# Recurrent mixer: output and low-rank products over the whole array, output norm over rows of tokens

## The chip, the cores and the metric

The kernel runs on one core of one Trainium2 chip. The metric is device time in microseconds. The kernel before took 5264.46 us, the median of three runs (5259.58 to 5285.39). The chip is driven by five engines that each work through their own queue in order and meet at semaphores: TensorE (PE, with its weight loads as PEld), VectorE (DVE), ScalarE (ACT), GpSimd (POOL) and SyncE (SP), which issues DMAs.

## The reference, cut to what matters

The program is a first block of hybrid layers and a second block with a differential attention, a recurrent mixer and a routed feed-forward part. The change touches the recurrent mixer alone: a scan over 256 context and 512 image tokens in two directions, 16 heads of 64, then a norm of each head's output.

```python
def rwkv_prepare(z, shift_w, w0, w_up, a0, a_up, k_k, k_a):
    ...
    r, k, v, wd, ad, gd = jnp.split(z, RW_SPLIT_IDX, axis=-1)
    w_log = -jax.nn.softplus(-(w0[...] + jnp.einsum('btr,drc->dbtc', jnp.tanh(wd), w_up))) - 0.5
    a = jax.nn.sigmoid(a0[...] + jnp.einsum('btr,drc->dbtc', ad, a_up))
    ...

def wkv_scan(s0, scan_in):
    def step(s, inp):
        w, kk, a, k, v, r = inp
        sa = jnp.einsum('dbhij,dbhj->dbhi', s, kk)
        s = s * w[..., None, :] - sa[..., :, None] * (kk * a)[..., None, :] + v[..., :, None] * k[..., None, :]
        return s, jnp.einsum('dbhij,dbhj->dbhi', s, r)
    return lax.scan(step, s0, scan_in)

def rwkv_post(y, r, k, v, gd, g_up, r_k, ln_g, ln_b):
    mu = jnp.mean(y, axis=-1, keepdims=True)
    var = jnp.mean(jnp.square(y - mu), axis=-1, keepdims=True)
    yn = ((y - mu) * lax.rsqrt(var + RW_LN_EPS)).reshape(B, T, C) * ln_g + ln_b
    bonus = jnp.sum(hs(r) * hs(k) * r_k, axis=-1, keepdims=True) * hs(v)
    return (yn.astype(r.dtype) + bonus.reshape(B, T, C)) * (jax.nn.sigmoid(gd) @ g_up)
```

`wd` and `ad` have 64 channels each, so the two low-rank products contract over 64. The mean and the variance are over the 64 channels of a head, for each token.

## The kernel before, in words

The function `rwkv_phase` is a stage of its own between two barriers. It works on units: 8 channel tiles `g` (128 channels, two heads) times 2 directions `d`, so 16 units `u = 2 g + d`. The 768 tokens are cut into 12 chunks of 64, of which the last 8 are image tokens with outputs. Inside a chunk the recurrence is solved with triangular products (`solve`, with X, Y, U and the matrix wAT), and from chunk to chunk a state wS is carried (`scan`).

The order is written out by hand. An outer loop runs iterations -2 to 17, an inner one 36 slots `k`, and every engine walks the same two loops and issues what its functions say for a slot. In iteration `i` unit `i` is built (`solve`, `fill`), unit `i-1` is scanned, unit `i+1` is prepared (low-rank products, exponentials), and in odd iterations from 3 on the tile `g = (i-3)/2` is finished (`final_product`, `final_steps`, `finals`). In even iterations the bonus, v and the key norm of a tile are computed. Nothing but this order and the semaphores decides when an instruction starts; an instruction that waits holds back all that stands behind it on its engine.

What a slot holds on TensorE: four products of `solve` (L1891 for U, L1902 for Z, or L1874 for the gram matrices in slots 0 to 2), then in slots 3 to 11 four of `fill` (L1917, L1922, L1927), then a piece of the scan. The scan takes three slots a chunk: slot 0 of the three gives W (L1942, and L1945 from wS), slot 1 gives N (L1949), slot 2 the new state (L1964, L1967) and, for the 8 image chunks, the output: L1958 from qr, L1959 from C (a part of the tile `gate_rows` in the profile) and L1970 from D. These three have 64 columns of weights, one for each token of the chunk, and write partitions 0 to 63 of bank 6. ACT copies W and N out (L2088, L2091) and U (L2072), DVE makes wS from the bank and the decayed wP (L2203, the first of a unit L2206) and does masked copies and transposes (L2215 to L2255). In slots 24 and 35 DVE takes four chunks of outputs over to `rows` (in the profile `y_rows`, 64 partitions x 1024: token in the chunk x chunk and channel), a copy for direction 0 (L2266), an addition for direction 1 (L2269).

The low-rank products (L1988) stand in slots 0, 2, 4 and 6. The weights of w lie in partitions 0 to 63 of `up` and those of a in 64 to 127, so each product contracts over 64 rows; ACT opens them with a sigmoid (L2121), and DVE sums the logs with a scan (L2278) in slot 3.

The output norm works on channels in partitions. In slot 9 eight transposes turn `rows` to 128 channels x 512 tokens (L2032), DVE copies it (L2354), a product with a block matrix of ones gives each head's sum in all its channels (L2037, slot 12), DVE subtracts (L2358) and squares (L2362), a second such product gives the variance (L2042, slot 16), ACT takes the root (L2167, slot 17), DVE two reciprocals (L2367, slots 18 and 20) and the product (L2370), then the scale and shift (L2373), the bonus (L2377) and the gate (L2383).

In the profile, tiles that lie in reused memory bear that memory's name: `x` stands for yb, sq, rk and ob, `arena` for the constants, up, wb, wk, wq and wV.

Of the kernel before, what the change touches and what calls it, by code (L numbers as in the profile page):

```python
# [11 lines left out]
ALU = mybir.AluOpType  # L12
# [3 lines left out]
P = 128  # L16
D = 1024
# [1717 lines left out]
def rwkv_phase(nc, T, R, lora, gd, ob_d):  # L1735
# [16 lines left out]
    bonus, rk, rows, yb, sq, ob = R["bonus"], R["rk"], R["rows"], R["yb"], R["sq"], R["ob"]  # L1752
# [26 lines left out]
    def r_slot(u):  # L1779
        return 1 + u % 3  # L1780

# [22 lines left out]
    def solve_step(k):  # L1804
# [6 lines left out]
             "s_ready", "y_ready", "norm_sums", "bonus_sums", "v_turned", "rows_turned", "mean_ready", "var_ready",  # L1811
             "gate_ready",
             "opened", "exps_ready", "q_widened", "y_preset", "u_copied", "bt_copied", "kt_copied", "w_copied",
             "n_copied", "s_copied", "s_decayed", "squared", "norm_roots", "v_copied", "ln_root",
             "sums_ready", "less_ready", "b_ready", "a_ready", "k_ready", "q_ready", "r_ready", "wb_ready", "wk_ready",
             "pl_ready", "y_opened", "at_ready", "d_ready", "x_opened", "x_done", "y_back", "y_final", "gram_k_read",
             "y_taken", "kr_ready", "kk_ready", "rk_ready", "bonus_ready", "yb_ready", "centred", "sq_ready",
             "normed", "inverse_ready", "ln_inverse", "scaled", "added", "ob_ready"]
    with Phase(nc, names) as (
            block, rk_loaded, v_loaded, up_loaded, ob_stored0, ob_stored1,  # L1820
            lora_up, gram_b, gram_k, b_turned, k_turned, u_ready, z_ready, w_ready, n_ready,
            s_ready, y_ready, norm_sums, bonus_sums, v_turned, rows_turned, mean_ready, var_ready,
            gate_ready,
            opened, exps_ready, q_widened, y_preset, u_copied, bt_copied, kt_copied, w_copied,
            n_copied, s_copied, s_decayed, squared, norm_roots, v_copied, ln_root,
            sums_ready, less_ready, b_ready, a_ready, k_ready, q_ready, r_ready, wb_ready, wk_ready,
            pl_ready, y_opened, at_ready, d_ready, x_opened, x_done, y_back, y_final, gram_k_read,
            y_taken, kr_ready, kk_ready, rk_ready, bonus_ready, yb_ready, centred, sq_ready,
            normed, inverse_ready, ln_inverse, scaled, added, ob_ready):
        ob_stored = (ob_stored0, ob_stored1)  # L1830

# [26 lines left out]
        def _(pe):  # L1858
# [71 lines left out]
            def scan(k, u):  # L1930
# [91 lines left out]
            def final_product(k, g, u):  # L2022
                if k == 9:
                    pe.wait_ge(y_taken, 4 * (g + 1))
# [10 lines left out]
                elif k == 12:  # L2035
                    pe.wait_ge(yb_ready, g + 1)
# [1141 lines left out]
```

## Time and profile before

| | |
|---|---|
| median of three runs | 5264.46 us |
| the profiled execution | 5262.22 us, span 5260.4 us |
| TensorE busy | 4544.4 us, 86% |
| DVE busy | 3151.8 us, 60% |
| ACT busy | 1603.0 us, 30% |
| POOL busy | 753.5 us, 14% |
| the mixer's stage | about 2408 to 3561 us of the span |
| granted clock, mean | 0.934 |

The page counts an engine busy only in its own instructions. A matmul in four-byte numbers is two passes, each with its weight load, so a group "x8" in the timeline is four products. Passes overlap at their ends, so a step is read from one start to the next and not from the durations. Slot 0 of the odd iteration read below starts at 2761.56 us, that of the next at 2830.88 and of the one after at 2899.09. The rows of idle time in brackets say what released the engine.

### The profile page before, as it was taken

To read this page: it belongs to the slowest core of one execution; us is meant where nothing else is said; L and a number is where in the kernel's file an instruction comes from. 1 tells how busy PE (TensorE), PEld (TensorE's weight loads), DVE (VectorE), ACT (ScalarE), POOL (GpSimd) and SP (SyncE) were. 2 spreads that over 40 slices of the span, in tenths; PEclk is the share of its full clock that TensorE was granted. 3 is DMA by queue.
4 is the path that set the end of the run, shared out by engine and by line. 5 is a ranking of instruction groups with operands and counts; after the bars stand their busy time and mean duration, and the time that the engine had idled before them with its cause. 6 is when DMAs were issued, how large, how long until landed. Compare 5 with 4: busy or idle time off the path is not lost. (4 is left out here: it accounts for less than half of the span.)

```text
span 5260.4 us, 56898 instructions
## 1 busy us (share of the span) xinstructions
PE 4544.4 (86%) x20568; PEld 3189.7 (61%) x20568; DVE 3151.8 (60%) x6333; ACT 1603.0 (30%) x3153; POOL 753.5 (14%) x671
## 2 busy tenths in 40 slices
PE   7978998978998997697999999998977777887787
PEld 5636886744885575486888888876763333333333
DVE  5563223564222557656677777743548888888886
ACT  3233342333432224213445444533211111111111
POOL 0000010000110000100000000001004445444443
PEclk9978999978999899898999999998989899989889
DMA  3102332201334410230000000005229999999998
GB/s 117 35 0 80 96 96 71 64 0 46 100 97 181 178 34 1 86 112 30 10 12 12 12 12 12 3 3 168 87 78 422 417 411 414 415 404 417 410 411 356
DMA packets 141383, 777.70 MB, mean 148 GB/s; under 512 B 18692, under 2 KB 23188, under 8 KB 73000
## 3 DMA queue, kind: packets, MB, share of 16 engines
q0 software_dynamic: 80224, 565.16, 26.3%
q1 hardware_dynamic: 60872, 208.82, 12.1%
q8 instruction: 168, 2.75, 0.2%
q14 instruction: 119, 0.97, 0.1%
HBM read 753.99 MB, written 19.92 MB: 147 GB/s over the span
## 5 line engine op out<-in xcount | busy, mean ns | idle before, releaser
L2809 PE MATMUL psum<-rows,diag 128*128 128x512 f32 x2048 | 1019.7, 656 | 296.5 <-ACT diag L2788 295.1
L2809 PEld LDWEIGHTS psum<-rows,diag 128*128 128x128 f32 x2048 | 420.2, 211 | 877.7 <-issue 877.4
L419 DVE TENSOR_TENSOR w_split_lo<-w_raw,w_split_hi 128x1024 fp32r<-128x1024 f32 (+1 forms) x316 | 379.4, 1209 | 648.5 <-ACT w_split_hi L406 644.1
L2699 POOL DMA_INDIRECT rows<-in_peer_uv,sel_idx x512 | 618.0, 1207 | 933.8 <-PE psum L2809 636.4
L2714 DVE SCALAR_TENSOR_TENSOR uh<-rows,h_rows 128x1024 f32<-128x1024 f32 x512 | 628.0, 1227 | 181.0 <-DMA rows<-in_peer_uv,sel_idx 152.0
L406 ACT CAST w_split_hi<-w_raw 128x1024 fp32r<-128x1024 f32 (+1 forms) x316 | 322.6, 1028 | 824.5 <-PE psum L357 457.7
L2781 ACT ACTIVATE g<-g 128x4 f32<-128x4 f32 x128 | 26.3, 205 | 1077.0 <-DVE g L2725 1077.0
L592 POOL TENSOR_TENSOR uT_lo<-normed_rows,uT_hi 128x512 fp32r<-128x512 f32 x64 | 82.9, 1295 | 1377.1 <-ACT uT_hi L568 1377.1
L1891 PE MATMUL psum<-X_wide,wAT_wide 128*128 128x128 f32 x1920 | 262.6, 280 | 1.9 <-DVE X_wide L2235 1.9
L1891 PEld LDWEIGHTS psum<-X_wide,wAT_wide 128*128 128x128 f32 x1920 | 235.1, 192 | 35.1 <-issue 30.9
L1902 PE MATMUL psum<-U_wide,Y_wide 128*128 128x128 f32 x1536 | 206.0, 277 | 0.0
L357 PE MATMUL psum<-hT_mlp_hi,w_split_hi 128*128 128x512 f32 x512 | 199.5, 390 | 2.2 <-DVE hT_mlp_lo L239 2.2
L1902 PEld LDWEIGHTS psum<-U_wide,Y_wide 128*128 128x128 f32 x1536 | 188.0, 192 | 19.0 <-issue 18.7
L357 PE MATMUL psum<-hT_mlp_lo,w_split_hi 128*128 128x512 f32 x512 | 199.2, 389 | 0.0
L357 PE MATMUL psum<-hT_mlp_hi,w_split_lo 128*128 128x512 f32 x512 | 199.2, 389 | 0.0
L357 PE MATMUL psum<-w_split_hi,uT_hi 128*128 128x512 f32 x512 | 199.2, 389 | 0.0
L357 PE MATMUL psum<-w_split_lo,uT_hi 128*128 128x512 f32 x512 | 199.2, 389 | 0.0
L357 PE MATMUL psum<-w_split_hi,uT_lo 128*128 128x512 f32 x512 | 199.2, 389 | 0.0
L2072 ACT COPY U_wide<-psum 128x512 f32<-128x512 f32 x240 | 140.6, 586 | 188.4 <-PE psum L1891 185.0
L2203 DVE SCALAR_TENSOR_TENSOR wS<-psum,pl,wP 128x128 f32<-128x128 f32 x160 | 54.9, 343 | 205.0 <-PE psum L1967 205.0
L2788 ACT ACTIVATE diag<-ident_sb,g 128x128 f32<-128x128 f32 x512 | 163.5, 390 | 36.7 <-DVE g L2730 36.7
L2432 POOL DMA_DIRECT2D merge_stage<-hT_spill x8 | 4.3, 539 | 1180.4 <-POOLq L168 1173.0
(492 smaller groups left out, 9291.2 us busy)
## 6 DMA issues: line engine op xcount, KB each, us to landing
w_raw<-in_w_in SPq DMA_DIRECT2D x120, 512.0 KB, 4.7
w_raw<-in_w_up SPq DMA_DIRECT2D x64, 512.0 KB, 4.5
w_raw<-in_w_down SPq DMA_DIRECT2D x64, 512.0 KB, 4.4
wbuf_mod<-in_w_mod SPq DMA_DIRECT2D x12, 2048.0 KB, 12.5
w_raw<-in_w_out SPq DMA_DIRECT2D x24, 512.0 KB, 5.0
w_raw<-in_peer_wq SPq DMA_DIRECT2D x16, 512.0 KB, 4.8
rows<-in_peer_uv,sel_idx POOLq DMA_INDIRECT x512, 13.0
w_raw<-in_w_branch_a SPq DMA_DIRECT2D x8, 512.0 KB, 4.6
```

The lines of the kernel that those rows point to most:

```text
L357: last = nc.tensor.matmul(psum[0:rows, bank, 0:cols], l_, r_, start=(start and c == 0 and j == 0), stop=(stop and c == len(pairs) - 1 and ...
L406: nc.scalar.copy(ring.hi[:, q % SPLIT_RING, :, 0:w], raw[:, q % raw_ring, :, 0:w]).then_inc(hi_ready, 1)
L419: nc.vector.tensor_tensor(ring.lo[:, q % SPLIT_RING, :, 0:w], raw[:, q % raw_ring, :, 0:w], ring.hi[:, q % SPLIT_RING, :, 0:w].bitcast(F32 ...
L592: return nc.gpsimd.tensor_tensor(uT.lo[:, k, :], squares[:, k % 2, :], uT.hi[:, k, :].bitcast(F32), ALU.subtract)
L1891: last = nc.tensor.matmul(psum[:, b, i * P:(i + 1) * P], flat(wAT[:, c]), flat(X[:, c]), start=True, stop=True)
L1902: last = nc.tensor.matmul(psum[:, b, i * P:(i + 1) * P], l_, r_, start=True, stop=True)
L2072: nc.scalar.copy(flat4(U[:, batch(b)]), psum[:, b, :]).then_inc(u_copied, 1)
L2203: nc.vector.scalar_tensor_tensor(wS[:], psum[:, 5, 0:P], scale, wP[:], ALU.mult, ALU.add).then_inc(s_copied, 1)
L2699: nc.gpsimd.indirect_dma_start(out=rows[:, n % RB, :], out_offset=None, in_=I["peer_uv"], in_offset=bass.IndirectOffsetOnAxis(ap=sel[:, t, ...
L2714: nc.vector.scalar_tensor_tensor(prod[:], rows[:, n % RB, 0:D], 1.0, h[:, t, :], ALU.mult, ALU.mult, accum_out=dots[:, (n // BATCH) % 2, s ...
L2788: nc.scalar.activation(diag[:, n % (2 * BATCH), :], ident[:], ACT.Copy, scale=g2[:, b % 2, i:i + 1]).then_inc(diag_ready, 1)
L2809: last = nc.tensor.matmul(psum[:, 2 * (t % 2) + half, :], diag[:, n % (2 * BATCH), :], rows[:, n % RB, D + half * NB:D + (half + 1) * NB], ...
```

## The change

Three things are done.

The three output products of a chunk get 128 columns of weights: those of the chunk and of the one behind it in memory (`two`). So qr, C and D get room for one chunk more, which POOL sets to zero at the stage's start; D moves to a tile of its own (`D_wide`). The products write all 128 partitions of bank 6, of which only the first 64 are read, as before.

The low-rank products contract over 128 rows: the weights of w are followed by 64 rows of zeros and those of a preceded by them, laid out so by the host, and `up` and its DMA have twice the size.

The output norm is taken on `rows`, with tokens in partitions, ahead of the transposes: sums of 64 columns by a DVE reduction (slot 1), times -1/64 (slot 2), added by a broadcast over rows (slot 3), squared on ACT (slot 4), reduced again (slot 6), root of the 64 x 16 statistics on ACT (slot 10), reciprocal (slot 11), product over rows (slot 14). The eight transposes then stand in slot 15, and the scale and shift reads their bank (slot 17). The two products with ones are gone. The gate product stays in slot 19.

```diff
+    def two(ap, u, c):
+        return ap[:, u % 2, c:c + 2].rearrange("p c t -> p (c t)")
...
+            nc.gpsimd.memset(qr[:, :, N_ALL:], 0.0).then_inc(pads_zero, 1)
...
-                        yy = psum[0:L_CH, 6, (x_ % 4) * P:(x_ % 4 + 1) * P]
-                        at = slice(c * L_CH, (c + 1) * L_CH)
+                        yy = psum[:, 6, (x_ % 4) * P:(x_ % 4 + 1) * P]
+                        at = slice(c * L_CH, (c + 2) * L_CH)
                         nc.tensor.matmul(yy, qr[:, r_slot(u), at], wS[:], start=True, stop=False)
-                        nc.tensor.matmul(yy, Cc[:, u % 2, x_], v, start=False, stop=False)
+                        nc.tensor.matmul(yy, two(Cc, u, x_), v, start=False, stop=False)
...
-                        last = nc.tensor.matmul(yy, Dd[:, u % 2, x_], wN[:], start=False, stop=True)
+                        last = nc.tensor.matmul(yy, two(Dd, u, x_), wN[:], start=False, stop=True)
...
-                nc.tensor.matmul(psum[:, 7, 0:hi - lo], up[64 * w:64 * w + 64, d, :], lora[64 * w:64 * w + 64, lo:hi],
-                                 start=True, stop=True).then_inc(lora_up, 1)
+                nc.tensor.matmul(psum[:, 7, 0:hi - lo], up[:, w, d, :], lora[:, lo:hi], start=True, stop=True
+                                 ).then_inc(lora_up, 1)
...
             def final_product(k, g, u):
-                if k == 9:
-                    pe.wait_ge(y_taken, 4 * (g + 1))
+                if k == 15:
+                    pe.wait_ge(rows_normed, g + 1)
...
-                elif k == 12:
-                    nc.tensor.matmul(psum[:, 7, :], cst["ones"][:], yb[:], start=True, stop=True
-                elif k == 16:
-                    nc.tensor.matmul(psum[:, 7, :], cst["ones"][:], sq[:], start=True, stop=True).then_inc(var_ready, 1)
                 elif k == 19:
-                    pe.wait_ge(ln_root, g + 1)
+                    pe.wait_ge(scaled, g + 1)
...
+                if k == 4:
+                    act.wait_ge(rows_centred, g + 1)
+                    nc.scalar.activation(rowsq, rows[:], ACT.Square).then_inc(rows_squared, 1)
+                elif k == 10:
+                    nc.scalar.activation(lnst[:, 3, :], lnst[:, 2, :], ACT.Sqrt, bias=cst["ln_eps"][0:L_CH],
...
+                if k == 1:
+                    nc.vector.reduce_sum(lnst[:, 0, :], grouped, AX.X).then_inc(row_sums, 1)
+                elif k == 3:
+                    nc.vector.tensor_tensor(grouped, grouped, each(lnst[:, 1, :]), ALU.add).then_inc(rows_centred, 1)
+                elif k == 6:
+                    nc.vector.reduce_sum(lnst[:, 2, :], rowsq.rearrange("p (g e) -> p g e", e=L_CH), AX.X
+                elif k == 14:
+                    nc.vector.tensor_tensor(grouped, grouped, each(lnst[:, 0, :]), ALU.mult).then_inc(rows_normed, 1)
+                elif k == 17:
                     dve.wait_ge(rows_turned, g + 1)
-                    nc.vector.tensor_copy(yb[:], psum[:, 7, :]).then_inc(yb_ready, 1)
...
-                    nc.vector.tensor_scalar(yb[:], yb[:], prm[:, g, 7:8], prm[:, g, 8:9], ALU.mult, ALU.add
+                    nc.vector.tensor_scalar(yb[:], psum[:, 7, :], prm[:, g, 7:8], prm[:, g, 8:9], ALU.mult, ALU.add
```

How the instructions move is seen in three places. The first is DVE's queue in slots 1 to 4 of an odd iteration, before the change (the run of masked copies and masks of the second and third block, then the first state wS, then the log sum of the next unit).

```order
L2223 STREAM_TRANSPOSE X_wide<-Y_wide 128x512
L2215 COPY_PREDICATED Y_wide<-arena,psum 128x512
L2217 TENSOR_TENSOR wAT_wide<-psum,arena 128x512
L2220 TENSOR_TENSOR gate_rows<-psum,arena 128x256
L2223 STREAM_TRANSPOSE X_wide<-Y_wide 128x512
L2206 TENSOR_SCALAR wS<-psum,pl 128x128
L2246 TENSOR_TENSOR wBT_wide<-psum,arena 128x512
L2278 SCALAR_TENSOR_TENSOR Lc_tile<-arena,dec_tile 128x768
L2282 TENSOR_TENSOR dec_tile<-Lc_tile,dec_tile 128x768
L2203 SCALAR_TENSOR_TENSOR wS<-psum,pl,wP 128x128
L2235 COPY_PREDICATED X_wide<-arena,psum 128x512
```

The same place after it; line numbers are those of the changed kernel, where L2223, L2225, L2231 and L2214 are the L2215, L2217, L2223 and L2206 of before.

```order
L2231 STREAM_TRANSPOSE X_wide<-Y_wide 128x512
L2366 TENSOR_REDUCE ln_stats<-y_rows 64x16
L2223 COPY_PREDICATED Y_wide<-arena,psum 128x512
L2225 TENSOR_TENSOR wAT_wide<-psum,arena 128x512
L2228 TENSOR_TENSOR D_wide<-psum,arena 128x256
L2231 STREAM_TRANSPOSE X_wide<-Y_wide 128x512
L2214 TENSOR_SCALAR wS<-psum,pl 128x128
L2369 TENSOR_SCALAR ln_stats<-ln_stats 64x16
L2254 TENSOR_TENSOR wBT_wide<-psum,arena 128x512
L2286 SCALAR_TENSOR_TENSOR Lc_tile<-arena,dec_tile 128x768
L2373 TENSOR_TENSOR y_rows<-y_rows,ln_stats 64x1024
L2290 TENSOR_TENSOR dec_tile<-Lc_tile,dec_tile 128x768
```

The reduction of `rows` now stands ahead of the third block's copy and of the first state, the small product with -1/64 behind the state, and the addition over `rows` between the log sum and the subtraction. The second place is TensorE's queue around the transposes of `rows`, before the change in slot 9.

```order
L1967 MATMUL psum<-wN,wbt_wide 128x128
L1891 MATMUL psum<-X_wide,wAT_wide 128x128 x4
L1917 MATMUL psum<-qr,arena 128x128 x4
L1942 MATMUL psum<-arena,wBT_wide 128x128
L1945 MATMUL psum<-wS,arena 128x128
L2032 MATMUL psum<-ident_sb,y_rows 128x64 x8
L1891 MATMUL psum<-X_wide,wAT_wide 128x128 x4
L1922 MATMUL psum<-ident_sb,arena 128x128 x4
L1949 MATMUL psum<-wW,Y_wide 128x128
L1891 MATMUL psum<-X_wide,wAT_wide 128x128 x4
```

After it, in slot 15 (L1902, L1956 and L1960 are the L1891, L1945 and L1949 of before, L1913 the L1902).

```order
L1980 MATMUL psum<-wN,wbt_wide 128x128
L1983 MATMUL psum<-wN,D_wide 128x128
L1902 MATMUL psum<-X_wide,wAT_wide 128x128 x4
L1953 MATMUL psum<-arena,wBT_wide 128x128
L1956 MATMUL psum<-wS,arena 128x128
L2045 MATMUL psum<-ident_sb,y_rows 128x64 x8
L1902 MATMUL psum<-X_wide,wAT_wide 128x128 x4
L1960 MATMUL psum<-wW,Y_wide 128x128
L1902 MATMUL psum<-X_wide,wAT_wide 128x128 x4
L1971 MATMUL psum<-wS,qr 128x128
```

The transposes have moved behind the last of the second level's Z products and an output product, to the third W product after; what stood between the two places is now ahead of them.

The third is ACT's queue in slots 4 to 6, before the change.

```order
L2078 COPY wbt_wide<-psum 128x512
L2091 COPY wN<-psum 128x128
L2095 ACTIVATE wP<-wS,pl 128x128
L2121 ACTIVATE aa_tile<-psum,arena 128x512
L2072 COPY U_wide<-psum 128x512
L2081 COPY wkt_wide<-psum 128x512
L2088 COPY wW<-psum 128x128
L2121 ACTIVATE aa_tile<-psum,arena 128x256
```

After it; L2100, L2126, L2077, L2086 and L2093 are the L2095, L2121, L2072, L2081 and L2088 of before.

```order
L2083 COPY wbt_wide<-psum 128x512
L2096 COPY wN<-psum 128x128
L2100 ACTIVATE wP<-wS,pl 128x128
L2126 ACTIVATE aa_tile<-psum,arena 128x512
L2172 ACTIVATE x<-y_rows 64x1024
L2077 COPY U_wide<-psum 128x512
L2086 COPY wkt_wide<-psum 128x512
L2093 COPY wW<-psum 128x128
L2126 ACTIVATE aa_tile<-psum,arena 128x256
```

The square of `rows` now stands ahead of the copies of U and of wkt in slot 5, without a table load before it.

## Rows read from the trace of the kernel before

**Rows 1.** Busy us in one stretch: PE, PEld, DVE, ACT, POOL; clock, DMA, GB/s.
```profile
2780.00:2850.00 70.00, 67.16 (x505) 57.68 (x504) 50.33 (x80) 33.24 (x74) 0.00 (x0) 1.00 0.01 5
```

**Rows 2.** TensorE's timeline, slots 19 to 22: start, us, engine, line, out<-in, shapes, count.
```profile
2803.11 1.02 PE L2045 MATMUL psum<-gd,arena 128*128 128x512 f32 x2
2803.97 1.05 PE L1902 MATMUL psum<-U_wide,Y_wide 128*128 128x128 f32 x8
2804.96 0.43 PE L1958 MATMUL psum<-wS,qr 128*64 128x128 f32 x2
2805.23 0.38 PE L1959 MATMUL psum<-arena,gate_rows 128*64 128x128 f32 x2
2805.54 0.49 PE L1964 MATMUL psum<-arena,wkt_wide 128*128 128x128 f32 x2
2805.86 0.39 PE L1967 MATMUL psum<-wN,wbt_wide 128*128 128x128 f32 x2
2806.18 0.43 PE L1970 MATMUL psum<-wN,gate_rows 128*64 128x128 f32 x2
2806.54 1.16 PE L1891 MATMUL psum<-X_wide,wAT_wide 128*128 128x128 f32 x8
2807.54 0.39 PE L1942 MATMUL psum<-arena,wBT_wide 128*128 128x128 f32 x2
...
2807.99 1.06 PE L1891 MATMUL psum<-X_wide,wAT_wide 128*128 128x128 f32 x8
2808.88 0.39 PE L1949 MATMUL psum<-wW,Y_wide 128*128 128x128 f32 x2
```

**Rows 3.** TensorE's timeline around one low-rank product.
```profile
2762.50 0.44 PE L1942 MATMUL psum<-arena,wBT_wide 128*128 128x128 f32 x2
2762.87 1.12 PE L1988 MATMUL psum<-lora,arena 64*128 64x512 f32 x2
2763.93 1.16 PE L1874 MATMUL psum<-qr,arena 128*128 128x128 f32 x8
```

**Rows 4.** Groups by line and shape: count, busy us, mean ns, idle before.
```profile
L1360 DVE TENSOR_REDUCE x<-head_squares 128x16 f32<-128x1024 f32 x10 | 12.1, 1211 | 0.0
...
L2367 DVE RECIPROCAL x<-x 128x256 f32<-128x256 f32 x16 | 27.4, 1720 | 3.0 <-ACT x L2167 3.0
...
L1336 ACT ACTIVATE head_squares<-arena 128x1024 f32<-128x1024 f32 x6 | 6.3, 1054 | 1.9 <-DVE arena L2864 1.9
...
L1964 PEld LDWEIGHTS psum<-arena,wkt_wide 128*128 128x128 f32 x352 | 52.7, 189 | 19.2 <-issue 19.2
...
L1958 PEld LDWEIGHTS psum<-wS,qr 128*64 128x64 f32 x256 | 24.5, 134 | 17.3 <-DVE y_rows L2266 2.6
```

**Rows 5.** TensorE's timeline, slot 3, the W product behind the first state.
```profile
2769.79 0.49 PE L1945 MATMUL psum<-wS,arena 128*128 128x128 f32 x2 [0.32 <-DVE wS L2206]
```

**Rows 6.** DVE's timeline, slots 12 to 14.
```profile
2789.78 0.73 DVE L2235 COPY_PREDICATED X_wide<-arena,psum 128x512 f32<-128x512 uint32 x1 [0.54 <-PE psum L1902]
...
2793.98 0.68 DVE L2358 SCALAR_TENSOR_TENSOR x<-psum,x 128x512 f32<-128x512 f32 x1
...
2795.19 0.33 DVE L2203 SCALAR_TENSOR_TENSOR wS<-psum,pl,wP 128x128 f32<-128x128 f32 x1
...
2796.07 0.65 DVE L2362 TENSOR_TENSOR x<-x 128x512 f32<-128x512 f32 x1
```

**Rows 7.** TensorE's timeline, slot 27 of an odd and slot 33 of an even iteration.
```profile
2819.46 0.49 PE L1945 MATMUL psum<-wS,arena 128*128 128x128 f32 x2 [0.97 <-DVE wS L2203]
...
2896.39 0.49 PE L1942 MATMUL psum<-arena,wBT_wide 128*128 128x128 f32 x2
2897.03 0.49 PE L1945 MATMUL psum<-wS,arena 128*128 128x128 f32 x2
```

**Rows 8.** The timeline of all engines at the mixer's end.
```profile
3547.24 0.70 PE L2032 MATMUL psum<-ident_sb,y_rows 64*128 64x64 f32 x8 [0.77 <-DVE y_rows L2269]
...
3559.82 0.69 DVE L2383 TENSOR_TENSOR x<-x,psum 128x512 f32<-128x512 f32 x1
```

More of the change, by code:

```diff
@@ L1751, in rwkv_phase @@
     wS, wP, wW, wN, pl = R["wS"], R["wP"], R["wW"], R["wN"], R["pl"]
-    bonus, rk, rows, yb, sq, ob = R["bonus"], R["rk"], R["rows"], R["yb"], R["sq"], R["ob"]
+    bonus, rk, rows, yb, ob = R["bonus"], R["rk"], R["rows"], R["yb"], R["ob"]
+    rowsq, lnst = R["rowsq"], R["lnst"]
     def cells(ap):
@@ L2102, in widen_q @@
                 at = slice(64 * half, 64 * half + 64)
-                nc.scalar.copy(wq[at, u % 2, :, half, :], cells(qr[at, 0, :])).then_inc(q_widened, 1)
+                nc.scalar.copy(wq[at, u % 2, :, half, :], cells(qr[at, 0, 0:N_ALL])).then_inc(q_widened, 1)
             def preset(j, u):
@@ L2164, in final_steps @@
             def final_steps(k, g):
-                if k == 17:
-                    act.wait_ge(var_ready, g + 1)
-                    nc.scalar.activation(sq[:], psum[:, 7, :], ACT.Sqrt, bias=cst["ln_eps"][:], scale=1.0 / 64
-                                         ).then_inc(ln_root, 1)
+                if k == 4:
+                    act.wait_ge(rows_centred, g + 1)
+                    nc.scalar.activation(rowsq, rows[:], ACT.Square).then_inc(rows_squared, 1)
+                elif k == 10:
+                    act.wait_ge(row_vars, g + 1)
+                    nc.scalar.activation(lnst[:, 3, :], lnst[:, 2, :], ACT.Sqrt, bias=cst["ln_eps"][0:L_CH],
+                                         scale=1.0 / 64).then_inc(row_roots, 1)
             for i in ITERATIONS:
@@ L2844, in second_block_program @@
     gd = sbt("gd", [P, S])
-    arena = sbt("arena", [P, 13400])
+    arena = sbt("arena", [P, 13656])
     with ExitStack() as stage:
@@ L2923, in second_block_program @@
         cst = {n: share.take(list(I["rwc_" + n].shape)[1:]) for n in T["rwc_names"]}
-        R = {"cst": cst, "prm": share.take([DC, 10]), "up": share.take([2, P]), "gup": share.take([DC, P]),
+        R = {"cst": cst, "prm": share.take([DC, 10]), "up": share.take([2, 2, P]), "gup": share.take([DC, P]),
              "zr_d": z_d["r"], "zk_d": z_d["k"], "zv_d": z_d["v"]}
@@ L2995, in second_block_program @@
         R["ob"] = room[:, 2 * S:4 * S].rearrange("p (i n) -> p i n", i=2)
-        R["rk"], R["yb"], R["sq"] = (room[:, i * S:(i + 1) * S] for i in (4, 5, 6))
+        R["rk"], R["yb"] = (room[:, i * S:(i + 1) * S] for i in (4, 5))
+        R["rowsq"] = room[0:L_CH, 6 * S:8 * S]
+        R["lnst"] = sb("ln_stats", [L_CH, 4, 2 * XCH])
         room2 = T["gate_rows"][:].rearrange("p t d -> p (t d)")
-        R["C"], R["D"] = (room2[:, i * 2 * S:(i + 1) * 2 * S].rearrange("p (i c t) -> p i c t", i=2, t=L_CH)
-                          for i in range(2))
+        R["C"] = room2[:, 0:2 * (XCH + 1) * L_CH].rearrange("p (i c t) -> p i c t", i=2, t=L_CH)
+        R["D"] = sb("D_wide", [P, 2, XCH + 1, L_CH])
         rwkv_phase(nc, T, R, lora, gd, obT_d)
@@ L3127, in lay_out @@
     W = A["w_in_2"]
+    none = np.zeros((64, 2, DC * P), W.dtype)
     order = np.concatenate([W[:, :, 0:6144], W[:, :, 6400:8448]], axis=2)
@@ L3143, in lay_out @@
                                A["rw_ln_b_2"][0]], 1).reshape(DC, P, 9)),
-        "rw_up": c(np.concatenate([A["rw_w_up_2"][0].transpose(1, 0, 2), A["rw_a_up_2"][0].transpose(1, 0, 2)], 0)
-                   .reshape(P, 2, DC, P).transpose(2, 0, 1, 3)),
+        "rw_up": c(np.stack([np.concatenate([A["rw_w_up_2"][0].transpose(1, 0, 2), none], 0),
+                             np.concatenate([none, A["rw_a_up_2"][0].transpose(1, 0, 2)], 0)], 1)
+                   .reshape(P, 2, 2, DC, P).transpose(3, 0, 1, 2, 4)),
         "rw_gup": c(A["rw_g_up_2"][0].reshape(P, DC, P).transpose(1, 0, 2)),
```

66 lines of the change are left out of this document (32 added, 34 removed).

## The prediction

> **What bounds it now.** I read the page's shares first, then the stretches, then the timeline of one iteration of the recurrent mixer. The program is one core and the mixer runs from 2408 to 3561 us of its span; nothing else runs beside it, so a microsecond taken from it is one off the end. In that stage the reader is to see TensorE busy 67.16 of 70.00 us with DVE at 50.33, ACT at 33.24 and a granted clock of 1.00 (the upper of its two levels, 2.4 GHz) [rows 1]. TensorE is the bound, by its own queue: an iteration of 36 slots takes about 68 to 69 us and has no long idle stretch. But a share is a mean: DVE has 72% over the stretch and runs without a pause in some slots, and there its order decides (below). The sum is made against the profiled execution: 5262.22 us, span 5260.4, 2.2 us below the median of 5264.46.
>
> **The pace of TensorE, full and cut.** Products over the whole array start 0.22 us apart (two in the 0.45 us from 2807.54 to 2807.99) and a group of four takes 0.89 (2807.99 to 2808.88) [rows 2]. Around a product with 64 columns of weights it is slower. The slot from 2803.97 goes 0.99 for the group of four, then 0.27, 0.31, 0.32, 0.32, 0.36 for the five products of the scan, and 1.00 for the next group: 3.57 us up to 2807.54, where seven steps at the full pace are 0.89 + 5 x 0.22 + 0.89 = 2.88 [rows 2]. Every step into, inside or out of the narrow shape costs 0.05 to 0.14, though the narrow product does less. Difference 0.69 us.
>
> **The change, part by part.**
>
> (a) Output products with 128 columns. Eight slots of each scan have the three products; seven look like rows 2, the last (slot 35, nothing behind it in the scan) I take at 0.25. 7 x 0.69 + 0.25 = 5.1 us an iteration, for the 15 iterations that also build: 76 us. The added columns go to rows of the bank that nobody reads, and the copy out of it is still of 64 rows, so DVE pays nothing. In the last scan (no build) TensorE waits for the copies of the state at each hop; I count nothing there (0 to 5).
>
> (b) Low-rank products with 128 rows. 2762.50 to 2762.87 is 0.37 for a product that has 0.22 at full pace, the 512-wide product takes 1.06 against 0.86 for the full one at 2803.11, and the group after it is slowed as in rows 2, by 0.10 [rows 2, 3]: 0.15 + 0.20 + 0.10 = 0.45 each. Four an iteration, 15 iterations (the narrower ones taken alike): 27 us. The weights' DMA doubles from 128 KB; it is asked for an iteration early, so 0.
>
> The Trainium skill speaks against this part: "TensorE: Matmul & The Clock Gate", section "Why this matters for your kernels", gives a single matmul with 32 rows the same time as one with 128 and puts the gain in running several at once. By it (a) and (b) would be near zero. The rows above differ from that here, since what they show is a cost of the neighbours too.
>
> (c) Two ones products leave, 0.86 each (2803.11 to 2803.97) [rows 2], in the seven iterations that hold a final and a build: 12 us.
>
> (d) DVE and ACT of the output norm. Off DVE go the copy (0.69), the subtraction, the square, two reciprocals of 1.72 [rows 4] and the product, 6.2 us. On come four passes over 64 x 1024: none is in the trace. Bounds: the reduction of 128 x 1024 to 16 at 1.21 above [rows 4], and the 64 x 512 cut of it, half, below; I take 1.2, since time follows the free size. With three small ones of 16 columns (an estimate of 0.5 together) it is 5.3 us. So DVE's load is as before; what matters is where they stand. The skill's "VectorE: DVE Perf Modes", "Rules for kernel authors", calls the reduce the slowest DVE operation and advises restructuring. The row has it at 1.21, the price of any pass of that size; by the page alone the same sum would carry a longer stop in slot 1.
>
> (e) The tail. From the transposes at 3547.24 to the end of DVE's last product (3559.82 + 0.69) [rows 8] it is 13.3 us of pure chain. After: reduce, small, add, square, reduce, root, reciprocal, product, transposes, scale, gate product (2.1 us at the idle clock), multiply: about 11.3. Gain 2.
>
> Gross: 76 + 27 + 12 + 2 = 117 us.
>
> **What is late next.** TensorE's queue gets faster, and in these places it then meets DVE or ACT:
>
> - Slot 3, every iteration. TensorE already waits 0.32 for DVE's first state [rows 5]; DVE's run up to it starts after the previous output and is not shortened. The two low-rank products ahead of it save 0.9 that is lost again: 15 x 0.9 = 13.5.
> - Slot 1, seven iterations: the reduce stands in that same run ahead of the state: 1.15 each, 8. Behind it on DVE are the third block's masks and the state, which the scan's W product waits for.
> - Slot 4: ACT's Square waits for the centred rows, and behind it are the copies of U and of wkt, which TensorE needs for the next gram product. The Square has 1.05 [rows 4]. Bounds 0 and 1.7; TensorE is itself 1.15 late by then, so I take 0.5: 3.5.
> - Slot 15, seven iterations. DVE's block from 2789.78 ends its state copy at 2795.52, 5.7 later; without the subtraction at 2793.98 it is 5.1 [rows 6]. TensorE at full pace is there after 0.44 + 1.11 + 1.99 + 1.11 = 4.65. Then the transposes wait for the last row product: 2796.07 less 0.6 plus 1.2 is 6.9 after the zero, against 4.8. Wait 2.1, with the state's 0.5 in it. 7 x 2.1 and 0.5 for the first: 15. With the old order the transposes stood in slot 9 and waited for nothing.
> - Slot 27: the wait of 0.97 [rows 7] is DVE's and grows by the 0.7 that the slot saves, 8 odd iterations: 5.5.
> - Slot 33 of the even ones, behind the reciprocals of the key norm: 0.64 where the pace is 0.22 [rows 7]; what the last two slots save is lost: 0.9 x 7 = 6.5.
>
> Sum given back 52. Net 117 - 52 = 65: **5262 - 65 = 5197 us**.
>
> **Rivals.**
> - The new waits hardly show: a late TensorE lets DVE and ACT catch up, so that only the waits that show now (20 us: slots 3 and 33) grow: 5262 - 117 + 20 = 5165. For it: DVE at 72%; against it: rows 5 and 6 are in-order queues.
> - The row statistics cost more than their places: all of the first reduce, add and second reduce (3.6), the Square (1.05) and the Sqrt's table load at slot 10 (1.3) reach TensorE, with the 2.1 of slot 15: 7 x 8 = 56, and 32 of the other waits: 117 - 88 = 29, 5233. For it: DVE has no pause in slots 0 to 4; against: TensorE's own lateness covers part of each.
> - Padding gives nothing (the rule above): the slow steps belong to the place, not to the shape. Then gross is 14, waits 8 + 3.5 + 7 x 1.4 = 21: 5270, no change.
> - Slower: the weight load shows. A load of 64 columns takes 0.13, one of 128 0.19 [rows 4]; if the steps of rows 2 are loads that nothing covers, each of the 768 passes of (a) costs 0.058 more: +44, with the 27 of new waits of the norm and less 14: 5262 + 57 = 5319. It decides from the point where a slot of (a) saves less than 0.1 us (the rest, 41 against 52, is then a loss). Against it: at the full pace 128-column weights come every 0.11 us a pass, faster than the narrow ones.
>
> **From cases to numbers.** Forecast 0.59 (its own range 5170 to 5225), hidden waits 0.15, dearer statistics 0.13, no gain 0.08, slower 0.05. The range of 8 in 10 is 5160 to 5240. What a measurement can tell from no change is about 0.5%, 26 us: faster than 5238 is the forecast, the hidden waits and three quarters of the third case, 0.84; the same 0.11; slower 0.05.
>
> **What would show it.** Right: the scan's products of a y slot 0.22 apart and 2.9 us for the stretch of rows 2; the low-rank product 0.86; new idle time of TensorE before the first W product (about 2 us), before the transposes of the normed rows (up to 2) and the release of both by DVE; iterations of about 63 us (even) and 66 (odd). Wrong: the narrow steps unchanged with 128 columns (no gain), a lower granted clock in the stage, TensorE's waits over 8 us in an odd iteration, or a later start of the low-rank products.

## The result, and the profile after

The changed kernel took 5216.59 us (median of four runs, 5212.29 to 5219.81) beside 5266.03 for the kernel before (now the median of four); the ratio is 0.990 with a 95% interval of 0.9872 to 0.9927, which is 38 to 67 us. The forecast was 5197 with a range of 5160 to 5240: the time lies inside it and the change is faster, by 49 us between the medians where 65 were forecast. The profiled execution took 5219.48 us, span 5217.7, 42.7 below the one of before.

The page of the changed kernel, span and the engines' busy time:

```profile
span 5217.7 us, 56829 instructions
...
PE 4469.1 (86%) x20536; PEld 3204.8 (61%) x20536; DVE 3144.6 (60%) x6333; ACT 1604.5 (31%) x3161; POOL 751.5 (14%) x674
```

The share of TensorE is still 86%. What changed is seen in the timeline. The stretch that answers to [rows 2], slots 19 to 21 of an odd iteration (columns as there):

```profile
2923.74 1.02 PE L2050 MATMUL psum<-gd,arena 128*128 128x512 f32 x2
2924.60 1.05 PE L1913 MATMUL psum<-U_wide,Y_wide 128*128 128x128 f32 x8
2925.49 0.39 PE L1971 MATMUL psum<-wS,qr 128*128 128x128 f32 x2
2925.71 0.39 PE L1972 MATMUL psum<-arena,gate_rows 128*128 128x128 f32 x2
2925.93 0.39 PE L1977 MATMUL psum<-arena,wkt_wide 128*128 128x128 f32 x2
2926.16 0.39 PE L1980 MATMUL psum<-wN,wbt_wide 128*128 128x128 f32 x2
2926.38 0.39 PE L1983 MATMUL psum<-wN,D_wide 128*128 128x128 f32 x2
2926.60 1.06 PE L1902 MATMUL psum<-X_wide,wAT_wide 128*128 128x128 f32 x8
2927.50 0.39 PE L1953 MATMUL psum<-arena,wBT_wide 128*128 128x128 f32 x2
```

The narrow steps are gone. From 2924.60 the group of four takes 0.89, each of the five products 0.22, the next group 0.90: 2.90 us where it was 3.57, and 2.88 was the forecast.

Single passes show what the narrow shape cost. In the trace of before a pass starts 0.11 us behind the one ahead of it in either shape. Only at the border is it more: the first narrow pass comes 0.09 later than that, the one behind it 0.05, the first wide pass again 0.09 and the one behind it 0.10. A visit to the narrow shape costs 0.34 us, and the slot of [rows 2] has two. The low-rank product, the answer to [rows 3]:

```profile
2748.75 0.44 PE L1953 MATMUL psum<-arena,wBT_wide 128*128 128x128 f32 x2
2749.03 1.02 PE L2001 MATMUL psum<-lora,arena 128*128 128x512 f32 x2
2749.89 1.05 PE L1885 MATMUL psum<-qr,arena 128*128 128x128 f32 x8
```

0.28 into it and 0.86 for it, where it was 0.37 and 1.06. Pass by pass it is the same picture: 0.09 to 0.10 more at each of four steps (into the first pass, to the second, to the group behind, and to that group's second pass), and the same for the products with 256 columns as for those with 512. The first state of a unit now holds TensorE for longer, the answer to [rows 5]:

```profile
2888.57 0.49 PE L1956 MATMUL psum<-wS,arena 128*128 128x128 f32 x2 [2.22 <-DVE wS L2214]
```

And this is the place in slot 15 where the transposes now stand:

```profile
2914.13 0.49 PE L1956 MATMUL psum<-wS,arena 128*128 128x128 f32 x2 [0.55 <-DVE wS L2211]
2915.84 0.81 PE L2045 MATMUL psum<-ident_sb,y_rows 64*128 64x64 f32 x8 [1.23 <-DVE y_rows L2383]
2916.58 2.07 PE L1902 MATMUL psum<-X_wide,wAT_wide 128*128 128x128 f32 x8
2918.45 0.63 PE L1960 MATMUL psum<-wW,Y_wide 128*128 128x128 f32 x2
2918.88 1.45 PE L1902 MATMUL psum<-X_wide,wAT_wide 128*128 128x128 f32 x8
2920.16 0.39 PE L1971 MATMUL psum<-wS,qr 128*128 128x128 f32 x2
```

TensorE waits 0.55 for the state and 1.23 for the last product over rows, 1.78 in all where 2.1 was forecast. But then the group of four takes 1.87 us (2916.58 to 2918.45) and the next 1.28, where 0.89 is the pace. The granted clock falls in just this stretch; each row is a stretch of 1 us with the busy time of PE, PEld, DVE, ACT and POOL, the granted clock, the DMA share and GB/s:

```profile
2914.00:2915.00 1.00, 0.49 (x2) 0.30 (x2) 1.00 (x3) 0.27 (x1) 0.00 (x0) 1.00 0.00 0
2915.00:2916.00 1.00, 0.16 (x2) 0.16 (x3) 0.78 (x1) 0.00 (x0) 0.00 (x0) 1.00 0.00 0
2916.00:2917.00 1.00, 1.00 (x10) 0.88 (x10) 0.00 (x0) 0.00 (x0) 0.00 (x0) 0.64 0.06 16
2917.00:2918.00 1.00, 1.00 (x6) 1.00 (x6) 0.00 (x0) 0.00 (x0) 0.00 (x0) 0.50 0.00 0
2918.00:2919.00 1.00, 1.00 (x7) 1.00 (x6) 0.00 (x0) 0.31 (x1) 0.00 (x0) 0.50 0.00 0
2919.00:2920.00 1.00, 1.00 (x8) 1.00 (x8) 0.00 (x0) 1.00 (x4) 0.00 (x0) 0.65 0.00 0
2920.00:2921.00 1.00, 1.00 (x11) 1.00 (x11) 0.00 (x0) 0.84 (x2) 0.00 (x0) 1.00 0.00 0
```

The granted clock is 1.00 through the two waits and falls to 0.50, the lower of the two levels (1.2 GHz), once TensorE is busy again; the time at the lower level in these rows adds up to 3.4 us. The wait of slot 3 was followed by such a fall in six odd iterations and in one not. Iteration 5, behind a wait of 2.21, and iteration 7, behind the 2.22 shown above:

```profile
2757.00:2761.00 4.00, 3.83 (x28) 3.36 (x29) 4.00 (x6) 3.23 (x8) 0.00 (x0) 1.00 0.01 2
...
2889.00:2892.00 3.00, 3.00 (x16) 3.00 (x15) 3.00 (x4) 2.06 (x4) 0.00 (x0) 0.50 0.00 0
```

DVE's side of the norm, minimum, median and maximum in ns for eight instructions each:

```profile
L2366 DVE TENSOR_REDUCE ln_stats<-y_rows x8: 1165/1169/1211, 2619.3 to 3504.5; 64x16 f32<-64x1024 f32 x8
...
L2373 DVE TENSOR_TENSOR y_rows<-y_rows,ln_stats x8: 1187/1194/1216, 2625.1 to 3505.9; 64x1024 f32<-64x1024 f32 x8
...
L2386 DVE TENSOR_SCALAR x<-psum,arena x8: 800/802/811, 2657.3 to 3512.5; 128x512 f32<-128x512 f32 x8
```

The reduction and the pass over rows were taken at 1.2 and are 1.17 and 1.19. The scale that now reads the bank takes 0.80. And the end of the stage:

```profile
3503.74 0.68 DVE L2277 TENSOR_TENSOR y_rows<-y_rows,psum 64x512 f32<-64x512 f32 x1 [2.27 <-PE psum L1983]
...
3511.38 1.11 PE L2045 MATMUL psum<-ident_sb,y_rows 64*128 64x64 f32 x8 [7.67 <-DVE y_rows L2383]
...
3515.56 0.69 DVE L2396 TENSOR_TENSOR x<-x,psum 128x512 f32<-128x512 f32 x1 [1.50 <-PE psum L2050]
```

From the end of the output's copy (3504.42) to the end of the last product (3516.25) it is 11.8 us; 11.3 was forecast, against 13.3 before.

The start of slot 0 in each iteration gives a ruler that the rest of the program does not disturb. In the table the even and the odd iteration are iterations 10 and 9, and the sum runs from slot 0 of iteration 0 to slot 0 of iteration 15, so that it holds six of the seven odd iterations with a build and a final. The time of a run is its median, and the ratio is to the kernel before on the same chip.

| kernel | time us | ratio (95%) | even | odd | sum of 15 |
|---|---|---|---|---|---|
| before | 5264 to 5268 | | 68.20 | 69.33 | 1014.0 |
| changed | 5216.6 | 0.990 (0.9872 to 0.9927) | 63.60 | 69.27 | 975.5 |
| low-rank alone | 5246.6 | 0.9961 (0.9947 to 0.9974) | 67.08 | 68.36 | 999.0 |
| output products alone | 5219.8 | 0.9915 (0.9901 to 0.9928) | 64.71 | 67.39 | 973.1 |
| both of these | 5205.9 | 0.9882 (0.9866 to 0.9897) | 63.58 | 66.61 | 960.0 |
| norm over rows alone | 5270.0 | 1.001 (0.9996 to 1.0023) | 68.21 | 69.85 | 1018.9 |
| changed, waits filled | 5203.7 | 0.9867 (0.9845 to 0.9888) | 63.59 | 66.29 | 959.0 |
| changed, norm late | 5181.0 | 0.9828 (0.981 to 0.9846) | 63.58 | 63.15 | 939.2 |
| norm late, wk late | 5168.1 | 0.9802 (0.9784 to 0.982) | 63.40 | 62.10 | 929.7 |
| before, narrow products together | 5250.1 | 0.9957 (0.9941 to 0.9974) | 66.61 | 68.71 | 996.6 |

The first rows say it at once: the even iterations got 4.6 us shorter, the odd ones, in which the norm stands, hardly at all (0.06). Not every odd iteration of the changed kernel is like the ninth: iterations 3 to 13 took 70.65, 67.81, 69.20, 69.27, 69.27 and 69.08 us.

### The profile page after: what moved, and what is told of

The parts are those of the page before. It is cut to its first block and busy times, and to the rows that moved or that the text cites. A ratio compares the mean times of both kernels' runs of the same rounds, so it can differ in the third digit from the quotient of the medians.

```text
span 5217.7 us, 56829 instructions
## 1 busy us (share of the span) xinstructions
PE 4469.1 (86%) x20536; PEld 3204.8 (61%) x20536; DVE 3144.6 (60%) x6333; ACT 1604.5 (31%) x3161; POOL 751.5 (14%) x674
## 5 line engine op out<-in xcount | busy, mean ns | idle before, releaser
L1902 PE MATMUL psum<-X_wide,wAT_wide 128*128 128x128 f32 x1920 | 266.6, 284 | 1.7 <-DVE X_wide L2243 1.4
L1902 PEld LDWEIGHTS psum<-X_wide,wAT_wide 128*128 128x128 f32 x1920 | 248.8, 200 | 17.5 <-issue 13.6
L1913 PE MATMUL psum<-U_wide,Y_wide 128*128 128x128 f32 x1536 | 202.2, 275 | 0.0
L1913 PEld LDWEIGHTS psum<-U_wide,Y_wide 128*128 128x128 f32 x1536 | 188.8, 192 | 7.5 <-issue 6.5
L2077 ACT COPY U_wide<-psum 128x512 f32<-128x512 f32 x240 | 140.1, 584 | 165.1 <-PE psum L1902 161.5
```

What stands on the lines that cost most here:

```text
L1902: last = nc.tensor.matmul(psum[:, b, i * P:(i + 1) * P], flat(wAT[:, c]), flat(X[:, c]), start=True, stop=True)
L1913: last = nc.tensor.matmul(psum[:, b, i * P:(i + 1) * P], l_, r_, start=True, stop=True)
L2077: nc.scalar.copy(flat4(U[:, batch(b)]), psum[:, b, :]).then_inc(u_copied, 1)
```

## The experiments

**The output products alone.** Of the diff only these lines, with the zeroed room behind qr, C and D that they need.

```diff
-                        yy = psum[0:L_CH, 6, (x_ % 4) * P:(x_ % 4 + 1) * P]
-                        at = slice(c * L_CH, (c + 1) * L_CH)
+                        yy = psum[:, 6, (x_ % 4) * P:(x_ % 4 + 1) * P]
+                        at = slice(c * L_CH, (c + 2) * L_CH)
...
-                        nc.tensor.matmul(yy, Cc[:, u % 2, x_], v, start=False, stop=False)
+                        nc.tensor.matmul(yy, two(Cc, u, x_), v, start=False, stop=False)
...
-                        last = nc.tensor.matmul(yy, Dd[:, u % 2, x_], wN[:], start=False, stop=True)
+                        last = nc.tensor.matmul(yy, two(Dd, u, x_), wN[:], start=False, stop=True)
```

> The kernel before with the output products at 128 columns of weights and nothing else. Theory A (the ledger: narrow products slow TensorE's queue by 0.69 us a slot, waits on DVE take some of it back, the full change lost its last 20 us to the norm and to falls of TensorE's clock after its waits): gross 76, given back about 16 in slots 15, 27 and 33, so 60 us faster than before, about 5204, faster than the whole change; no stretch at the lower clock in the odd iterations; even and odd iterations both near 64.5 us. Theory B (each part gives its share of the 46 measured, padding 40 of it): 40 faster, about 5225.

44 us faster, not 60. The steps of 0.22 are there and, in iterations 3 to 14, the full clock, and the whole change is not better than this part alone (5219.8 and 5216.6). The expected 64.5 came for the even iterations; the odd ones have 67.4. There TensorE meets DVE in slots in which the forecast had no wait. TensorE's waits in the second half of an odd iteration, slots 21, 26 and 27:

```profile
2931.15 0.49 PE L1955 MATMUL psum<-wS,arena 128*128 128x128 f32 x2 [0.43 <-DVE wS L2215]
...
2934.42 0.49 PE L1970 MATMUL psum<-wS,qr 128*128 128x128 f32 x2 [0.77 <-DVE y_rows L2278]
...
2938.35 0.49 PE L1955 MATMUL psum<-wS,arena 128*128 128x128 f32 x2 [1.43 <-DVE wS L2215]
```

The first (0.43) stands behind the reciprocals of the old norm, the second (0.77) waits for the copy that empties the output bank, the third (1.43) for the state. Together 2.6 us, where the forecast had one wait of 1.67 in slot 27. Set beside the trace of before product by product, an even iteration here gains 4.9 us in its eight output slots and gives 1.4 back to waits; the odd one gives back about 3.0 of the same gain. Theory B's number was nearer here, but its reasoning (parts that add up) does not fit the ruler: the three parts alone are 41, 15 and -5 us in the sum of 15 iterations, together 51, and the changed kernel has 38.5. In the times the two cannot be told apart (44, 17 and -6 make 55, within the interval of 38 to 67).

**The low-rank products alone.**

```diff
-                nc.tensor.matmul(psum[:, 7, 0:hi - lo], up[64 * w:64 * w + 64, d, :], lora[64 * w:64 * w + 64, lo:hi],
+                nc.tensor.matmul(psum[:, 7, 0:hi - lo], up[:, w, d, :], lora[:, lo:hi], start=True, stop=True
```

> The kernel before with the low-rank products over 128 rows and nothing else. Theory A: 27 us gross, the half that stands ahead of slot 3's W product is lost to the wait for DVE's first state, which grows from 0.32 to about 1.2 us: 12 to 14 faster, about 5252. Theory B (a product over 64 rows has the price of one over 128, and only the steps around it count): 4 to 6 faster, about 5260, with the 512-wide product itself still at 1.06 us.

15 us less in the sum of 15 iterations and a ratio of 0.9961, which is 20 us with an interval of 14 to 28 (the medians differ by 17). The profiled execution was the slowest of the five (5266.8), so only the mixer's stage is read from it. TensorE's wait for the first state in this kernel:

```profile
2900.69 0.49 PE L1945 MATMUL psum<-wS,arena 128*128 128x128 f32 x2 [0.89 <-DVE wS L2206]
```

0.89 where it was 0.32: 0.57 of what the two products ahead of it saved is lost in that wait, as (b) had it. Each iteration gains 1.0 to 1.1 us; 0.9 was the forecast. Theory B's numbers are out: the gain is three to four times as large, and the 512-wide product now has 0.86 by its starts. Its thought is not: the 0.20 that the product is shorter is 0.10 and 0.09 at the border of its two passes, the same for 512 and for 256 columns, so this too can be a price of changing shape rather than of a product over 64 rows. No run has such products one behind the other.

**The norm over rows alone.** The statistics on rows, the transposes in slot 15 and no ones products, as in the diff of the change; the paddings left out.

> The kernel before with the output norm over rows of tokens and nothing else. Theory A: 12 us of ones products and 2 of the tail go, the waits in slots 3 and 15 cost 8 + 3 + 8, and TensorE's clock falls to half after them in most of the seven odd iterations, 1.5 us each time: 5 to 25 us slower than before, 5270 to 5290. Theory B (the norm over rows is worth its two products, the whole change lost its time elsewhere): 5 to 12 faster, about 5256.

0.1% slower with an interval from no change to 0.2%: the lower end of theory A's time, and against theory B's 5 to 12 us faster. But theory A had the clock fall in most of the seven odd iterations, and that did not happen: five of the six in the ruler are 0.5 us longer than before (69.85) at a clock of 1.00. One is 71.35, and in that one the granted clock was 0.90 from 3320 to 3330 and 0.95 from 3330 to 3345; iteration 15, behind the ruler, has a fall too. At the old pace the waits are 1.43 in slot 3 (was 0.31) and 1.23 in slot 15, and slot 27 has 0.71 (was 0.96): 2.1 us more of waiting, where two ones products of 0.86 leave.

**Both paddings, old norm.** The two diffs above.

> Both paddings, with the output norm of before. Theory A: 60 + 13 = 73 faster than before, about 5191, 25 under the whole change, odd iterations near 64 us where the whole change has 69.2, and a clock of 1.00 throughout. Theory B (the norm over rows costs nothing and the paddings alone give what the whole change gives): about 5220, the same as the whole change or slower.

62 us faster by the ratio (58 between the medians), not 73, but faster than the whole change with its third part; the sum of the 15 iterations is 15.5 us shorter than that of the changed kernel. The expected 64 us of the odd iterations are 66.6, by the same three waits of slots 21, 26 and 27 (here 0.43, 0.77 and 1.44). Theory B is out: taking the norm over rows away from the change gives time back.

**The waits of the changed kernel filled.** Products of the identity with itself, into a part of the output's bank that is free there, in the iterations that hold a build and a final.

```diff
+    FILL_AT = {3: 9, 15: 2}
...
+                    if build is not None and final is not None and k in FILL_AT:
...
+                        for _ in range(FILL_AT[k]):
+                            nc.tensor.matmul(psum[:, 6, 3 * P:4 * P], ident[:], ident[:], start=True, stop=True)
...
                 if k == 15:
+                    if u is not None:
+                        for _ in range(5):
+                            nc.tensor.matmul(psum[:, 6, 3 * P:4 * P], ident[:], ident[:], start=True, stop=True)
```

> The changed kernel with products of the identity that nobody reads laid into TensorE's two waits of an odd iteration: 9 ahead of slot 3's W product, 2 ahead of slot 15's and 5 ahead of the transposes, 16 in all and 3.6 us of TensorE's time, no more than the 4.0 us that it waits there. Theory A (the waits are followed by a fall of the granted clock from 2.4 to 1.2 GHz, and it is this fall that eats the rest of the forecast): the odd iterations go from 69.2 to about 66.3 us, clock 1.00 in all of them, 15 to 20 us faster than the changed kernel, about 5198. Theory B (the clock falls for another reason, or costs nothing since DVE sets the pace): odd iterations stay at 69.2 or get longer by what the added products take, 5216 to 5225.

The kernel does 107 products more than the changed one (16 in each of six iterations, 11 in the last, which has no transposes' five) and is faster: 5203.7, ratio 0.9867, 13 us below the changed kernel where 15 to 20 were expected, and 16.5 us less in the sum of 15 iterations. All six odd iterations with a final in the ruler have 66.29 us. The timeline of TensorE in slot 15, with the filling (L2040) ahead of the transposes (L2049):

```profile
2910.50 0.49 PE L1957 MATMUL psum<-wS,arena 128*128 128x128 f32 x2
2910.83 1.28 PE L2040 MATMUL psum<-ident_sb 128*128 128x128 f32 x10
2912.21 0.71 PE L2049 MATMUL psum<-ident_sb,y_rows 64*128 64x64 f32 x8
2912.85 1.16 PE L1903 MATMUL psum<-X_wide,wAT_wide 128*128 128x128 f32 x8
2913.84 0.39 PE L1961 MATMUL psum<-wW,Y_wide 128*128 128x128 f32 x2
```

The group behind the transposes takes 0.99 where it took 1.87. The granted clock around the two places (stretch, length, busy times, clock, DMA share, GB/s):

```profile
2883.00:2890.00 7.00, 6.79 (x55) 6.12 (x54) 7.00 (x11) 3.68 (x8) 0.00 (x0) 1.00 0.01 2
...
2912.00:2916.00 4.00, 3.89 (x37) 3.72 (x37) 0.16 (x1) 1.96 (x5) 0.00 (x0) 1.00 0.00 0
```

It is 1.00 in both, and the trace has no stretch at the lower level from iteration 3 to 15. So theory A holds on its main point: it was the lower clock after the waits, not the waits alone, that took what the forecast had counted as gain. The size, too: 69.27 less 66.29 is 3.0 us an odd iteration. The changed kernel's iteration 5, whose clock fell behind slot 15 alone, splits it: 67.81 less 66.29 is 1.5 us for that fall, and 69.27 less 67.81 is 1.5 for the one behind slot 3.

**The norm later in the iteration.** Only slot numbers are changed.

```diff
             def final_product(k, g, u):
-                if k == 15:
+                if k == 23:
...
-                elif k == 19:
+                elif k == 29:
...
             def finals(k, g):
-                if k == 1:
+                if k == 5:
...
-                elif k == 14:
+                elif k == 21:
```

> The changed kernel with the steps of its output norm in other slots and nothing else: sum in slot 5 (was 1), mean 8 (2), centring 10 (3), square 12 (4), second sum 15 (6), root 17 (10), reciprocal 18 (11), product 21 (14), transposes 23 (15), scale 26 (17), bonus 28 (25), gate product 29 (19), last product 31 (27). Theory A (the norm over rows costs by where its steps stand in DVE's queue): the wait in slot 3 goes from 2.2 to 1.1 us, the one of 1.8 in slot 15 to 0.3 or less, no fall of the clock, odd iterations at 65.5 to 66 us, 23 to 26 us faster than the changed kernel, about 5192, and below both paddings alone (5206). Theory B (the steps cost what DVE is busy with them, wherever they stand): new waits of the same size in slots 21 to 27, 5205 to 5220.

5181.0, ratio 0.9828, 25 us below both paddings alone and 36 below the changed kernel; more than the 23 to 26 expected. The odd iterations are now the shorter ones, 63.15. TensorE's waits for DVE from slot 15 on, the last row being slot 3 of the next:

```profile
2901.43 0.49 PE L1956 MATMUL psum<-wS,arena 128*128 128x128 f32 x2 [0.55 <-DVE wS L2211]
...
2921.18 0.49 PE L1956 MATMUL psum<-wS,arena 128*128 128x128 f32 x2 [0.78 <-DVE wS L2211]
...
2940.09 0.49 PE L1956 MATMUL psum<-wS,arena 128*128 128x128 f32 x2 [0.70 <-DVE wS L2214]
```

Slot 15 keeps 0.55 for the state, the transposes wait for nothing, slot 27 has 0.78, and slot 3 of the odd iterations has 1.10 where it had 2.22. The waits of slots 21 and 26, which came with the old norm, are not there, as in the changed kernel. The granted clock is 1.00 in all of iterations 3 to 13. So of the 36 us in the sum of 15 iterations, 16.5 are what the filled kernel also had back, and the other 20 are shorter waits. Theory B is out.

**And wk later.**

```diff
-                elif k in (23, 24):
-                    h = k - 23
+                elif k in (27, 28):
+                    h = k - 27
```

> The kernel of the late norm with DVE's two products for wk in slots 27 and 28 (were 23 and 24), where it has no solve work. Theory A: the waits for DVE in slots 26 and 27 (0.8 and 1.4 us in the odd iterations) fall to near nothing, 10 to 16 us faster than the late norm, about 5180; the wait of 0.84 in slot 33 of the even iterations may grow by some tenths, as the key norm's reciprocals stand behind them. Theory B (the two slots are late because TensorE's own work ahead is short, not because DVE is behind): no more than 4 us faster.

5168.1 us, ratio 0.9802: 13 us below the last one and the fastest of all, 48 below the changed kernel. In the odd iteration no wait of slots 21 to 27 is left. As expected the even ones keep theirs in slot 33 (0.83). Theory B, no more than 4 us, is out.

**The narrow products together.** The kernel before, with another order inside a slot.

```diff
                         nc.tensor.matmul(yy, qr[:, r_slot(u), at], wS[:], start=True, stop=False)
                         nc.tensor.matmul(yy, Cc[:, u % 2, x_], v, start=False, stop=False)
+                        pe.wait_ge(n_copied, 12 * u + n + 1)
+                        last = nc.tensor.matmul(yy, Dd[:, u % 2, x_], wN[:], start=False, stop=True)
...
                         nc.tensor.matmul(S_, flat(wkt[:, u % 2, c]), v, start=True, stop=False)
...
-                    if n >= CCH:
-                        last = nc.tensor.matmul(yy, Dd[:, u % 2, x_], wN[:], start=False, stop=True)
```

> The kernel before with its three narrow output products one behind the other, ahead of the two state products (before: two, the state products, one), so that TensorE goes into the narrow shape once in a slot and not twice. Theory A (what costs is the change of shape: about 0.1 in and 0.1 to 0.14 out, twice a slot): the seven steps of a slot take about 3.3 us in place of 3.57, 0.25 to 0.3 less in some 105 slots, of which the waits leave 15 to 25 us, about 5243. Theory B (what costs is each narrow product by itself): 3.57 stays and so does the time, 5260 to 5266, or a little slower since the new state comes 0.3 us later.

TensorE's timeline in one such slot, where L1961 is the L1970 of before:

```profile
2804.40 1.06 PE L1891 MATMUL psum<-X_wide,wAT_wide 128*128 128x128 f32 x8
2805.39 0.43 PE L1958 MATMUL psum<-wS,qr 128*64 128x128 f32 x2
2805.66 0.38 PE L1959 MATMUL psum<-arena,gate_rows 128*64 128x128 f32 x2
2805.88 0.38 PE L1961 MATMUL psum<-wN,gate_rows 128*64 128x128 f32 x2
2806.19 0.49 PE L1968 MATMUL psum<-arena,wkt_wide 128*128 128x128 f32 x2
2806.51 0.39 PE L1971 MATMUL psum<-wN,wbt_wide 128*128 128x128 f32 x2
2806.74 1.06 PE L1902 MATMUL psum<-U_wide,Y_wide 128*128 128x128 f32 x8
2807.63 0.39 PE L1942 MATMUL psum<-arena,wBT_wide 128*128 128x128 f32 x2
```

0.99, 0.27, 0.22, 0.31, 0.32, 0.23, 0.89: 3.23 us for the seven steps, where [rows 2] had 3.57 and the wide products have 2.90. The same narrow products, entered once and not twice, cost half of the difference: one visit of 0.34 in place of two. Between the second and the third narrow product it is 0.22, the full pace. So it is the change of shape that is paid for, going in and coming out, and the ratio of 0.9957 (22 us, interval 14 to 31) shows it in the time. Theory B is out.

## Why the prediction was right, and where it was too large

- **(a) The output products.** The mechanism and the price of a slot were right: 3.57 to 2.90, forecast 2.88. One reading was too wide: steps inside the narrow shape cost nothing (0.22 a product); what looked like it is the second pass behind the border. Gross 76 with 16 given back makes 60; alone the part gives 44 (41 in the ruler). The gross was right (4.9 us an iteration, forecast 5.1), what was mis-sized are the waits: 1.4 us in an even and about 3.0 in an odd iteration, where 16 us in 15 iterations make 1.1. With the old norm, slots 21 and 26 (0.43 and 0.77) were missing; in the changed kernel these two waits do not show.
- **(b) The low-rank products.** 27 less 13.5 were forecast; 15 measured in the ruler. Going into the product was put at 0.15 above the full pace and costs 0.09 (0.37 against 0.28), so the gross is nearer 60 x 0.39 = 23 than 27. By its starts the product over 64 rows took 1.06 and over 128 takes 0.86. The Trainium skill, "TensorE: Matmul & The Clock Gate", section "Why this matters for your kernels", gives a single product with 32 rows the time of one with 128. This case does not refute that for the product by itself, since what the 64 rows add is the same for 512 and 256 columns; it shows that the padding was worth 15 us in the ruler all the same, where the rule as the forecast read it would have given near zero.
- **(c), (d) The norm.** DVE's load was about even (3144.6 us busy, 3151.8 before), and the places decided, as the text said: slot 3 waits 2.22 where the terms for slots 3 and 1 gave 0.32 + 0.9 + 1.15 = 2.37; slot 15 waits 1.78 where 2.1 stood; slot 27 1.38 where 1.67 stood; slot 33 0.84 where 1.3 stood. The Square of slot 4 was taken at 0.5; the wkt wait behind it is 0.39 with the clock up, none with it down.
- **The step that failed.** "Iterations of about 63 us (even) and 66 (odd)": the even ones are 63.6, the odd ones mostly 69.1 to 69.3. The forecast took the stage's clock of 1.00 [rows 1] as given and named a lower one only as a sign of being wrong. The new waits let it fall, and the 3 us that this costs in an odd iteration are 16.5 us in the sum of the filled kernel and 13 in its time, most of the 20 that the forecast of 5197 is off. The clock has no term in the sum, so that the time still lies in the stated range is owed to the range's width and not to the working. With the waits filled the odd iteration has 66.29: the walk through the slots, without the clock, was right to 0.3 us, though partly by errors that cancel (every wait was taken a little too long, and gains a little too high).
- **The tail.** 2 us forecast, 1.5 measured.
- **The rivals.** Padding that gives nothing and the weight load that shows are refuted by the 0.22 steps with 128 columns. Hidden waits are refuted by slots 3 and 15. The dear statistics (5233) came nearest in its total, but by luck: the waits of slots 3 and 15, 4.0 us together, stayed under the forecast's own terms (4.5), where this rival puts 8 us of the norm on top, and the clock, which it does not name, made up the rest. Its sum also does not add up as written: the other waits that it puts at 32 are 29 in the forecast's list (52 less 8 and 15).

What stays open: why the clock stayed up after the wait of slot 3 in iteration 5 (67.81 us, wait 2.21) and fell in the others, and what makes it fall at all. The length of the wait alone does not decide: at the new pace slot 27 waited 1.38 in the changed kernel, 1.43 with the output products alone and 1.44 with both paddings, and the clock stayed at 1.00.

## What to carry to other kernels

A product that uses half of the array's columns or rows costs its neighbours too: read the starts around it, and if its shape is alone among full ones, pad it with columns or rows that nobody reads, or at least put such products together. When the bounding engine gets faster, walk its queue slot by slot against the next engine's queue and move that engine's long steps to slots in which it has nothing urgent; here that was worth 36 and 13 us, where the two paddings gave 58. And price a new wait of TensorE with the clock that follows it.

## What the runs showed of the hardware

- 64-column products among 128-column ones: 0.34 us for each visit to the narrow shape (0.14 going in, 0.19 coming out), nothing between them; products 0.22 apart in either shape. Products over 64 rows among products over 128 (two passes): 0.09 to 0.10 at each of four steps, whether 256 or 512 columns stream through.
- In the changed kernel the granted clock fell from 2.4 to 1.2 GHz for 3.4 us (once for 6.8, in iteration 3) after TensorE had sat idle for 0.55 and 1.23 us with one product between, in six of six odd iterations, and after the wait of slot 3 (2.2, in the last odd iteration 2.88) in six of seven. After a wait of 0.60 in slot 15 of that last one it stayed at 1.00. A fall of 3.4 us cost about 1.5. With the old pace around them, waits of 1.43 and 1.23 (the norm alone) left it at 1.00 in the odd iterations of 69.85, and one of 71.35 showed 0.90. It fell from 0.2 us before the work resumed (iteration 3) to 1.5 us after it (iteration 13), so most of the lower clock lay on work and not on the wait.
- 107 products that nobody reads, put into waits, made the kernel 13 us faster (5216.6 to 5203.7).
- A tensor_scalar of 128 x 512 takes 0.80 us from the bank where it took 0.53 from SBUF; a plain copy from the bank had 0.69.
